# First layer's experts in four 32-row blocks per pass instead of two 64-row blocks, on TensorE's column quarters

## What is computed

```python
def _route(h, w_r, b_r):
    s = jax.nn.sigmoid(jnp.matmul(h, w_r, preferred_element_type=jnp.float32))
...
    _, idx = lax.top_k(jnp.where(emask, sb, -jnp.inf), TOP_K)      # 8 of 64
    w = jnp.take_along_axis(s, idx, axis=1)
    w = w / jnp.sum(w, axis=-1, keepdims=True) * ROUTED_SCALE
    return idx, w

def step(acc, blk):                       # _moe_routed, over blocks of tokens of one expert
    tok, w, e = blk
    xb = h_pad[tok]
    y = (jax.nn.silu(xb @ wg[e]) * (xb @ wu[e])) @ wd[e]
    return acc.at[tok].add(y * w[:, None].astype(y.dtype)), None
```

## Time and profile before

| what | value |
|---|---|
| time, median of 3 runs (lowest to highest) | 2921.68 us (2916.32 to 2924.86) |
| the profiled execution, its own time | 2924.61 us |
| its span, first to last instruction | 2922.8 us |
| TensorE busy (matmul) | 2597.2 us, 89% |
| DVE, ACT, POOL busy | 1081.2, 587.3, 389.9 us |
| DMA | 619.27 MB, mean 212 GB/s |
| mean granted TensorE clock | 0.953 |

### The profile page before, as it was taken

How to read it: one execution, slowest core, us unless ns; L and a number is a source line. 1 busy time by engine, 2 the same in 40 slices (tenths; PEclk the granted TensorE clock), 3 DMA queues, 4 the chain that set the end, 5 groups by cost and what they waited for, 6 DMA issues and landing times. The chain is left out here.

```text
span 2922.8 us, 44582 instructions
## 1 busy us (share of the span) xinstructions
PE 2597.2 (89%) x13635; PEld 1267.8 (43%) x13636; DVE 1081.2 (37%) x3197; ACT 587.3 (20%) x1379; POOL 389.9 (13%) x312
## 2 busy tenths in 40 slices
PE   6999989896899999999996588989978999899894
PEld 3566555543433333333332266656533333333331
DVE  3443360515333333333332643451433332233223
ACT  2323241402011111111111341331311111111111
POOL 1000001001021222221221200001010212121211
PEclk9999999997999999999998799999989999999997
DMA  7120303007478998999993402212155999998983
GB/s 276 47 91 30 125 20 129 30 15 285 161 240 301 351 324 288 320 329 333 327 367 78 190 1 90 87 40 89 37 222 226 370 398 392 385 390 286 389 309 106
DMA packets 104979, 619.27 MB, mean 212 GB/s; under 512 B 22832, under 2 KB 23088, under 8 KB 64688
## 3 DMA queue, kind: packets, MB, share of 16 engines
q1 hardware_dynamic: 71184, 530.30, 46.0%
q0 software_dynamic: 33696, 87.63, 12.3%
HBM read 578.84 MB, written 77.99 MB: 225 GB/s over the span
## 5 line engine op out<-in xcount | busy, mean ns | idle before, releaser
L1513 PE MATMUL ps<-wgu,xT 128*64 128x512 f32 x3584 | 809.4, 605 | 42.7 <-DMA wgu<-in_exp_gu 33.6
L1513 PEld LDWEIGHTS ps<-wgu,xT 128*64 128x64 f32 x3584 | 254.5, 139 | 502.5 <-issue 491.5
L1522 PE MATMUL ps<-wd,hiddenT 128*64 128x512 f32 x1824 | 418.3, 600 | 11.8 <-issue 11.5
L624 PE MATMUL ps<-w_in,hT 128*128 128x512 f32 (+5 forms) x1152 | 370.4, 481 | 14.9 <-PEq L574 3.8
L1442 POOL DMA_INDIRECT ffn_rows<-Y,six x114 | 182.6, 1602 | 1114.3 <-issue 663.2
L1695 DVE TENSOR_TENSOR hidden<-silu,ps 128x256 f32<-128x256 f32 x112 | 47.1, 421 | 705.2 <-ACT silu L1631 693.7
L624 PEld LDWEIGHTS ps<-w_in,hT 128*128 128x128 f32 x1152 | 217.6, 196 | 157.4 <-issue 138.2
L1522 PEld LDWEIGHTS ps<-wd,hiddenT 128*64 128x64 f32 x1824 | 122.7, 137 | 226.7 <-issue 226.7
L1631 ACT ACTIVATE silu<-ps 128x256 f32<-128x256 f32 x112 | 43.1, 384 | 798.6 <-PE ps L1513 798.6
L1626 ACT ACTIVATE Y<-ps,wc 128x512 f32<-128x512 f32 x114 | 78.4, 688 | 415.9 <-PE ps L1522 415.9
L1689 DVE TENSOR_SCALAR Y<-ps,wc 128x512 f32<-128x512 f32 x114 | 85.6, 750 | 197.0 <-PE ps L1522 197.0
(11 more groups left out here) (490 smaller groups left out, 2725.2 us busy)
## 6 DMA issues: line engine op xcount, KB each, us to landing
wgu<-in_exp_gu SPq DMA_DIRECT2D x128, 2048.0 KB, 22.6
wd<-in_exp_d SPq DMA_DIRECT2D x128, 1024.0 KB, 8.6
ada_start<-in_ada_w SPq DMA_DIRECT2D x8, 1024.0 KB, 7.9
w_in<-in_w_in SPq DMA_DIRECT2D x4, 2048.0 KB, 10.5
w_in<-in_w_out SPq DMA_DIRECT2D x4, 2048.0 KB, 12.7
aw_0A<-in_ada_w SPq DMA_DIRECT2D x6, 1024.0 KB, 4.9
aw_0B<-in_ada_w SPq DMA_DIRECT2D x6, 1024.0 KB, 4.8
aw_0C<-in_ada_w SPq DMA_DIRECT2D x6, 1024.0 KB, 4.8
```

The costliest lines, as they stand in the source:

```text
L624: last = pe.matmul(pp[i % 2][:, at:at + c1 - c0], hT[:, k, i * P:(i + 1) * P], wg[g % 2][:, k, c0:c1], start=(k == 0), stop=(k == KD - 1))
L1513: last = pe.matmul(ps[h * HB:(h + 1) * HB, 0, :], xT[:, k, h * HB:(h + 1) * HB], wgu[w[h]][:, k, :], start=(k == 0), stop=(k == KD - 1))
L1522: last = pe.matmul(ps[h * HB:(h + 1) * HB, 1 + c, :], G[:, f, h * HB:(h + 1) * HB], wd[w[h]][:, f, c * 512:(c + 1) * 512], start=(f == 0), ...
```

## The change

- `BLOCK = (P // 4, P // 2)`: the first layer's blocks have 32 rows, four a pass; the second layer keeps 64 rows, two a pass. `BPP` is the number of blocks in a pass. Constants that depend on it (thresholds, offsets) stand once per layer.
- Gate-up and down products are issued for four blocks, each on 32 columns. The word of a pass names the first buffer and for each further block whether its expert is the next one: `NB * 2 ** (BPP - 1)` texts, 40 in the first layer, 10 in the second.
- The table holds the experts of four blocks, for both layers by the same code; a spread table of experts by row (`ecol`) is made in `route` by TensorE.
- DVE in a pass: the offsets of each block (`cur`), one marking operation for all 128 rows, and the weight column by a compare with the row's expert and a sum over 64 entries, in place of copies per block. This goes for both layers.
- Four sets of result rows in the first layer, three to be filled with zeros (17 fills on SP instead of 5), four to be added in `ffn_residual`: GpSimd adds sets 2 and 3, DVE adds set 1 and then their sum.
- SP loads the gate-up weights of two experts ahead of the down weights in the first layer (`lead`), one in the second as before.

```diff
-HB = P // 2
+BLOCK = (P // 4, P // 2)
+MOST = P // min(BLOCK)
...
-                for i in range(nt - 1):
-                    sp.dma_start(v.acc_dram[NROW + i * P:NROW + (i + 1) * P, :], ex.Y[0][:, :]).then_inc(s_zero.sem, 16)
+                for i in range((BPP - 1) * nt - 1):
+                    at_row = (1 + i // nt) * NROW + i % nt * P
+                    sp.dma_start(v.acc_dram[at_row:at_row + P, :], ex.Y[0][:, :]).then_inc(s_zero.sem, 16)
...
+    HB = BLOCK[l]
+    BPP, at = P // HB, C_LAYER + l * C_SPAN
+    lead = BPP // 2
+    variants = NB * 2 ** (BPP - 1)
+    pairs = ((nt * P * 8 + E * HB) // HB + BPP - 1) // BPP
...
-                def gate_up_products(w, count):
-                    wait_weights(w_gu, w, count)
+                def gate_up_products(ws, count):
+                    wait_weights(w_gu, ws, count)
                     for k in range(KD):
-                        for h in range(2):
-                            last = pe.matmul(ps[h * HB:(h + 1) * HB, 0, :], xT[:, k, h * HB:(h + 1) * HB], wgu[w[h]][:, k, :],
+                        for h in range(BPP):
+                            last = pe.matmul(ps[h * HB:(h + 1) * HB, 0, :], xT[:, k, h * HB:(h + 1) * HB], wgu[ws[h]][:, k, :],
                                              start=(k == 0), stop=(k == KD - 1))
                     last.then_inc(gate_up, 1)
...
                     for f in range(2):
                         for c in range(2):
-                            for h in range(2):
+                            for h in range(BPP):
                                 last = pe.matmul(ps[h * HB:(h + 1) * HB, 1 + c, :], G[:, f, h * HB:(h + 1) * HB],
-                                                 wd[w[h]][:, f, c * 512:(c + 1) * 512], start=(f == 0), stop=(f == 1))
+                                                 wd[ws[h]][:, f, c * 512:(c + 1) * 512], start=(f == 0), stop=(f == 1))
...
+                def buffers(variant):
+
+                    ws = [variant // 2 ** (BPP - 1)]
+                    for h in range(1, BPP):
+                        ws.append((ws[-1] + variant // 2 ** (BPP - 1 - h) % 2) % NB)
+                    return ws
+
                 def by_buffers(word, products, count, a, n):
 
                     if n == 1:
-                        products((a // 2, (a // 2 + a % 2) % NB), count)
+                        products(buffers(a), count)
                         return
...
-                    by_buffers(was, down_products, was % VAR, 0, 2 * NB)
+                    by_buffers(was, down_products, was % VAR, 0, variants)
...
-                        by_buffers(now, gate_up_products, now % VAR, 0, 2 * NB)
+                        by_buffers(now, gate_up_products, now % VAR, 0, variants)
...
-                def weight_column(es, j):
-                    for h in range(2):
-                        half = slice(h * HB, (h + 1) * HB)
-                        dve.tensor_copy(wc[j][half, :], X[j][half, bass.ds(es[h] + D, 1)]).then_inc(wcol, 1)
+                def weight_column(i, j, done):
+                    dve.scalar_tensor_tensor(out=picked[:, :], in0=cst[:, C_IOTA:C_IOTA + E], scalar=ecol[:, bass.ds(i + 1, 1)], in1=X[j][:, D:HROW],
+                                             op0=ALU.is_equal, op1=ALU.mult).then_inc(step_s, 1)
+                    dve.wait_ge(step_s, done)
+                    dve.tensor_reduce(wc[j][:, :], picked[:, :], AX, ALU.add).then_inc(wcol, 1)
...
-                    sp.dma_start(f[:, i, :], v.acc_dram[i * P:(i + 1) * P, :]).then_inc(s_f[i].sem, 16)
-                    sp.dma_start(f2[:, i, :], v.acc_dram[NROW + i * P:NROW + (i + 1) * P, :]).then_inc(s_f[i].sem, 16)
+                    for h in reversed(range(BPP)):
+                        sp.dma_start(sets[h][:, i, :], v.acc_dram[h * NROW + i * P:h * NROW + (i + 1) * P, :]).then_inc(s_f[i].sem, 16)
...
+                def add_far_sets(i):
+                    s_f[i].wait(pool, 16 * BPP)
+                    pool.tensor_tensor(sets[2][:, i, :], sets[2][:, i, :], sets[3][:, i, :], ALU.add).then_inc(s_far.sem, 1)
...
                 def add_halves(i):
-                    s_f[i].wait(dve, 32)
-                    dve.tensor_tensor(f[:, i, :], f[:, i, :], f2[:, i, :], ALU.add).then_inc(s_sum.sem, 1)
+                    s_f[i].wait(dve, 16 * BPP)
+                    near = dve.tensor_tensor(f[:, i, :], f[:, i, :], sets[1][:, i, :], ALU.add)
+                    if BPP == 4:
+                        step(near)
+                        s_far.wait(dve, i + 1)
+                        near = dve.tensor_tensor(f[:, i, :], f[:, i, :], sets[2][:, i, :], ALU.add)
+                    near.then_inc(s_sum.sem, 1)
```

More of the change, by code:

```diff
@@ L1181, in _ @@
                     out = ps[:, 7, i * E:(i + 1) * E]
-                    pe.matmul(out, nbb[:, :], csth[0:E, H_TSTHB:H_TSTHB + E], start=True, stop=False)
+                    pe.matmul(out, nbb[:, :], csth[0:E, H_TSTHB + l * E:H_TSTHB + (l + 1) * E], start=True, stop=False)
                     for j in range(i):
@@ L1187, in _ @@
                 shared.gate_up_products(pe, 1, 1, 0 if half < KD else 3, KD)
+                s_eb.wait(pe, 1)
+                for h in range(BPP):
+                    last = pe.matmul(ps[h * HB:(h + 1) * HB, 7, 0:P], tb[:, h:h + 1].broadcast_to([P, HB]), v.ident, start=True, stop=True)
+                last.then_inc(s_ec.sem, 1)
                 s_tab.wait(pe, 1)
-                for c in range(3):
-                    last = pe.matmul(ps[0:1, 0, c * P:(c + 1) * P], tb[:, c:c + 1], v.ident, start=True, stop=True)
+                for c in range(BPP + 1):
+                    last = pe.matmul(ps[0:1, 5 + c // 4, c % 4 * P:(c % 4 + 1) * P], tb[:, c:c + 1], v.ident, start=True, stop=True)
                 last.then_inc(s_tt.sem, 1)
@@ L1308, in _ @@
[L1308 to L1314, removed]
+                word, e0, top, total, passes, turns = BPP, BPP + 1, BPP + 2, BPP + 3, BPP + 4, BPP + 5
@@ new lines, in _ @@
+                step(dve.tensor_scalar(col(word), col(e0), -float(NB), col(0), ALU.mult, ALU.add))
+                for h in range(1, BPP):
+                    step(dve.tensor_tensor(col(top), col(h), col(h - 1), ALU.subtract))
+                    step(dve.tensor_scalar(col(word), col(word), 2.0, col(top), ALU.mult, ALU.add))
+                step(dve.tensor_copy(col(total), ps[:, 0, E - 1:E]))
+                whole(col(passes), col(total), 1.0 / BPP, 0.5 - 0.5 / BPP)
+                whole(col(turns), col(total), 1.0 / (BPP * U), 0.5 - 0.5 / (BPP * U))
@@ L1756, in ffn_residual @@
         f = v.sb(f"f{l}", [P, nt, D], scope=scope)
-        f2 = v.sb(f"second{l}", [P, nt, D], scope=scope)
+        sets = [f] + [v.sb(f"set{h}_{l}", [P, nt, D], scope=scope) for h in range(1, BPP)]
         g2 = v.sb(f"g2_{l}", [P, streams, D], scope=scope)
@@ L1783, in _ @@
             def _(pool):
+                def add_far_sets(i):
+                    s_f[i].wait(pool, 16 * BPP)
+                    pool.tensor_tensor(sets[2][:, i, :], sets[2][:, i, :], sets[3][:, i, :], ALU.add).then_inc(s_far.sem, 1)
+                for i in range(min(2, nt) if BPP == 4 else 0):
+                    add_far_sets(i)
                 for i in range(nt):
+                    if BPP == 4 and i + 2 < nt:
+                        add_far_sets(i + 2)
                     s_ms.wait(pool, i + 1)
```

194 lines of the change are left out of this document (107 added, 87 removed).

## The result

| what | before | after |
|---|---|---|
| median, runs beside each other (lowest to highest) | 2923.27 us (2916.32 to 2928.72) | 4603.20 us (4592.05 to 4621.24) |
| ratio, 95% interval | | 1.576 [1.573, 1.579] |
| profiled execution, its span | 2924.61, 2922.8 us | 4621.24, 4619.3 us |

What follows compares the result with a forecast made beforehand. TensorE was taken to bound the first layer's loop. The profiled 2924.6 us, plus 1178 for text refetched in the loop and 14 for the rest, gave 4117 us, a median of 4114; range 3260 to 4680.

Steps and rivals of the forecast that it cites:

- Program text fetched again and again: First layer's loop: 33 packets of TensorE text don't stay, so jumps refetch them every pass; +1178 us, chance 0.90.
- The mis-sized term: First layer's loop: a pass of 34.9 us from 12.1 of work, 6 jumps and two clock drops; 1954 us for 56.
- The price of 3.27 us: First layer's loop: idle time per jump to missing text, the median of four gaps in the earlier trace.
- my 6: First layer's loop: jumps to missing text per pass, taken between 7.9 (5 packets stay) and 4.2 (16 stay).
- Route, +4: Before the first layer's loop: more DVE arithmetic in route, +2 us; together with twelve more row-set fills +4.
- End of the layer, +10: First layer's end: 24 loads instead of 12 and one more DVE addition per tile; +7 to +13 us, 10 taken.
- The low end's own terms: Range's low end: 2 jumps a pass at 3.1 us and one clock drop, 19.8 us a pass; 3260 us in all.
- Rival 1: First layer's loop: text stays once fetched, so fewer passes pay off; 2842 to 2934 us, chance 0.07.
- 2 (two quarters at a time): First layer's products: quarters run only two at a time, text held; 22.9 us a pass, 3440 us, chance 0.02.
- Rival 3: First layer's loop: fetches hide behind queued products, some 2 gaps a pass; 3260 us, 0.15 of the forecast's chance.
- Rival 4: First layer's loop: passes aren't cut, 64 remain with the new texts; 4400 us, chance 0.01.
- Second layer, nothing within 5: Second layer: same blocks, words and texts, DVE operations replaced by two of the same size; no change within 5 us.

Runs made afterwards that it cites:

- texts5w: The changed kernel with 5 product texts of each kind in the first layer instead of 40, waits in a separate tree, some sums wrong: 2910.82 us, ratio 0.997.
- apart4: The kernel before, with three more copies that never run behind each product text of the first layer: 4187.74 us (one run).
- joined5: The changed kernel with 5 texts of each kind, and one tree instead of two per product group, some sums wrong: 2887.46 us, ratio 0.989.
- lump: The kernel before, with forty product texts that never run placed between the down products and the turn of the hidden units: 3890.39 us, ratio 1.332.
- texts20: The changed kernel with 20 product texts of each kind in the first layer instead of 40, some sums wrong: 4239.15 us (one run).
- compact: The changed kernel, all sums kept, with compares and common parts side by side and the 80 product texts behind them, reached by jumps: 3529.55 us (one run).
- joined5d: joined5 with DVE adding all four sets of result rows at the first layer's end and GpSimd none: 2882.71 us, ratio 0.986.

## Why the prediction was right, and what was mis-sized

**The loop.** Program text fetched again and again was the forecast, and texts5w (text short, products kept: the 1680 us are gone) with apart4 (text long, nothing else changed: 1268 us lost) show it from both sides. The signs named ahead came: packets in every stretch of the loop, gaps at the three groups, a clock of 0.67, 59 marks on 768 columns. Of the 1696.5 us between the two spans 1669 lie in the loop (2465.8 against 796.7).

**The mis-sized term** is "12.1 + 6 x 3.27 + 2 x 1.6 = 34.9 us" a pass; it measured 44.0. Idle time was 26.8 us and not 6 x 3.27 = 19.6. The price of 3.27 us came from single gaps at a loop's entry and exit; in the loop gaps of 7.29 and 14.17 us stand where several far jumps follow each other (five compares that stand among the texts, then the text). Which factor was short can't be read from the rows, since they don't count jumps. By the walk that comes near the packets (below; 5.0 jumps a pass to a missing packet, as the expectation of the reordered kernel has it) it was the price, 26.8 / 5.0 = 5.4 us, and that my 6 lay so near was partly luck, for my walk lacked the packet that is brought along. The clock cost about 5 us a pass and not 3.2: gate-up products took 9.04 for 7.09 us, down products 5.66 for 3.65, and the turned rows 1.94 for 1.10, a third place that I had left out. I had also left out the fourth gap of the earlier trace rows, 2.42 us, behind which the group took its full-speed 3.65 us. What the rows do count is the packets, and over five kernels the time follows them:

| kernel | packets in the loop's text, at 234 records | fetched a pass | us a pass | over 12.45, per packet |
|---|---|---|---|---|
| before | 4.7 | 0 | 12.45 | |
| short text (joined5) | 5.9 | 0 | 13.2 | |
| lump | 12.9 | 7.2 | 27.5 | 2.1 |
| apart4 | 17.2 | 9.4 | 32.2 | 2.1 |
| texts20 | 17.4 | 10.5 | 37.5 | 2.4 |
| compact | 34.7 | 5.2 | 24.7 | 2.4 |
| after | 34.5 | 12.7 | 44.0 | 2.5 |

The loop's text is counted here with its compares, jumps and register steps, 1100 records before where the prediction had 1012. The 234 are matmuls and weight loads alone, so the first column of numbers is somewhat high, in all kernels alike. The last column is the time over 12.45 us divided by the packets fetched; with the 13.2 us of joined5 as the base, the three kernels of four blocks have 2.2 to 2.4. That packets cost the time is shown by these kernels together; the price is a ratio, in which idle time and clock aren't separated.

**What is kept.** I took 6 jumps by a walk in which the packets last touched stay and no others come. More arrives than such a walk allows, whatever its size: followed through its text, a pass of the changed kernel touches 8.2 different packets on average and one of the lump 5.6, and 12.7 and 7.2 arrive. So packets come that a pass never touches. The Trainium skill, Runtime: NRT & Kernel Launch, section Instruction fetch mechanics, calls TensorE's 128 KiB a FIFO, with the next page fetched while the current one runs. A walk by that rule, eight packets, first in first out, each entry bringing the next along, gives 13.2 packets a pass for the changed kernel, 10.1 for texts20, 9.8 for apart4, 0 to 9 for the lump by where packet borders fall, and 8.0 for compact. Three of the five are near the table, the lump lies within its span, and compact fetched fewer. Without the next packet brought along the same walk gives 6.3, 4.3, 3.6, none and 3.5, all under what was measured. That the first in goes out first is not shown: where the eight packets last touched stay and the next is brought along, the walk gives 13.5, 11.1, 10.6, 0 to 9 and 6.3, which is as near (averages over where packet borders fall).

The two-page window of that section is refuted here too, by the joined5 loop of 5.9 packets without a fetch. Where between 5.9 and 12.9 packets the fetching begins, and by what rule a packet is dropped, stays open: no loop of seven to ten packets was run, nor one whose texts are reached through a jump table instead of compares.

**Other terms.** Passes: 56, as said. Products doubled in number at no cost: 7.07 against 7.09 us, as said. Route, +4: first gate-up at 797.3 against 793.9 us, but six kernels with the same route stage have it at 791.7 to 798.7, so this term is within what one run differs from the next. End of the layer, +10: from the last down product to DVE's last operation 60.3 us (3263.15 to 3323.42) against 42.8 (1590.59 to 1633.40), +17.5. I had GpSimd's addition lying beside DVE's for nothing. In the changed kernel four DVE operations beside GpSimd's additions take 3.24 to 3.40 us instead of 1.22 to 1.28, and DVE waits for its sum twice, 2.30 us each. One of the four:

```profile
3290.32 2.35 POOL L1821 TENSOR_TENSOR set<-set 128x1024 f32<-128x1024 f32 x1 [1.63 <-DMA f<-ffn_rows]
3290.35 3.40 DVE L1841 TENSOR_TENSOR f<-f,set 128x1024 f32<-128x1024 f32 x1 [0.26 <-DMA f<-ffn_rows]
```

By the profiles of joined5 and joined5d, giving that addition to GpSimd saved nothing: the stage was 3 us longer with it.

Second layer, nothing within 5: the rest of the span, 1289.4 us before and 1295.9 after, +6.5; its loop is the same, and other kernels with this second layer have 1284.4 (texts20) to 1292.7 (compact). DMA near 120 GB/s: 102. The low end's own terms add up to 3268 us and not 3260, which changes nothing.

**The rivals.** Rival 1 (fetched once) and 2 (two quarters at a time) are refuted by the packets and by texts5w. Rival 3 (fetches hidden behind queued products) is refuted as a whole by 26.8 us of gaps a pass. Its remark that quarters leave a given queue half the time fits what stays once the text is held, 0.7 us a pass in joined5 and 1.2 with the second tree of texts5w. These two show that the steps between the products matter; that quarters cover them for only half as long is argued, not shown. Rival 4 (no fewer passes) is refuted by the 59 marks.

## What to carry to other kernels

Where a loop picks one of many written-out texts, count the loop's program text in packets before counting the work saved: a loop of 5.9 packets ran free here, one of 12.9 paid 15 us a pass, though nearly two thirds of it never ran. If the count can't shrink, change the order: with the compares and the common parts side by side and the texts behind them, the same text took 1074 us less. No version here beats the kernel before and computes all of its sums: joined5 and joined5d are 1.1 and 1.4% faster with 5 texts where 40 are needed.

## What the hardware showed that I had not expected

- Text that never runs, between two parts of a loop, is not free: 15.1 us a pass (lump).
- Per fetched packet a pass lost 2.1 to 2.5 us in five kernels, idle time and clock together, though their jumps are spread differently.
- An addition of two SBUF tiles on DVE takes 3.40 us instead of 1.23 when one on GpSimd runs beside it; with GpSimd's gone all take 1.22 or 1.23. The Trainium skill, SBUF — State Buffer, section Who interferes with whom, says that such an operation of DVE contends with GpSimd's reads, over a port pair that is locked exclusively. The rows agree: GpSimd's addition ends at 3292.67 us and DVE's 1.08 us behind it, at 3293.75, about as long as it takes alone.
